# Eleven adaLN weight slabs move from the two mixer stages into the dense gate-up stage

## What is computed

```
mod = silu(c) @ w_ada[l] + b_ada[l]           # 1024 -> 6144, per sequence (1 prompt, 8 samples)
sh1, sc1, gt1, sh2, sc2, gt2 = split(mod, 6)
h = rmsnorm(x, g_mix) * (1 + sc1) + sh1
y = token_mixers(h)                            # SSD | forgetting attention | gated DeltaNet | MoBA
x = x + gt1 * (y @ w_out)
h = rmsnorm(x, g_ffn) * (1 + sc2) + sh2
x = x + gt2 * ffn(h)                           # layer 0: dense SwiGLU, layer 1: top 2 of 8 experts
```

## Time and profile before

| | us |
|---|---|
| median of 3 runs | 1411.33 |
| lowest and highest | 1409.72, 1417.41 |
| span of the profiled execution | 1419.1 |
| TensorE busy in it | 1301.8 |
| VectorE busy | 941.5 |
| ScalarE busy | 707.7 |
| time of layer 0's attention loop to the last product with the cache | about 205 to 280 |
| dense layer (gate-up, then down) | about 345 to 542 |
| layer 1's attention loop | about 713 to 780 |

### The profile page before, as it was taken

How to read it: one execution, slowest core, us unless ns; L and a number is a source line. 1 busy time by engine, 2 the same in 40 slices (tenths; PEclk the granted TensorE clock), 3 DMA queues, 4 the chain that set the end, 5 groups by cost and what they waited for, 6 DMA issues and landing times.

```text
span 1419.1 us, 25438 instructions
## 1 busy us (share of the span) xinstructions
PE 1301.8 (92%) x10487; PEld 1126.2 (79%) x10487; DVE 941.5 (66%) x1612; ACT 707.7 (50%) x1188; POOL 10.1 (1%) x22
## 2 busy tenths in 40 slices
PE   4999898987999998998888878999999999999994
PEld 3899756766999997998666657888887979797984
DVE  1675635624555545676358247898899899989986
ACT  2566222214444444563132125776677677767772
POOL 0000000000000000000000000000000000000000
PEclk9999877588999999999776888999999999999997
DMA  9545358553444443456265523898889889979991
GB/s 388 213 154 207 121 183 318 180 215 149 178 179 141 164 186 130 175 202 202 62 226 163 188 110 125 324 358 304 320 336 347 301 324 351 335 281 343 349 339 39
DMA packets 30332, 326.76 MB, mean 230 GB/s; under 512 B 6018, under 2 KB 6530, under 8 KB 8066
## 3 DMA queue, kind: packets, MB, share of 16 engines
q1 hardware_dynamic: 28738, 319.17, 61.3%
q0 software_dynamic: 1472, 5.89, 1.1%
HBM read 319.15 MB, written 5.89 MB: 229 GB/s over the span
## 4 chain that ended last, share of the span: by engine, by line
PE 81%; DVE 9%; DMA 4%; ACT 3%; issue 3%; SPq 0%; DVEq 0%; POOL 0%; ACTq 0%; POOLq 0%
PE bank L747 19%; PE bank L748 18%; PE bank L749 18%; PE bank L1132 4%; DMA ring<-in_w_ada 4%; PE bank L667 3%; PE bank L803 2%; PE bank L1226 2%; PE bank L644 1%; PE bank L699 1%; DVE w_low L2400 1%; DVE win_low L1877 1%; PE bank L1254 1%; PE bank L1005 1%; PE bank L770 1%
## 5 line engine op out<-in xcount | busy, mean ns | idle before, releaser
L2400 DVE TENSOR_TENSOR w_low<-ring,w_high 128x1024 fp32r<-128x1024 f32 x352 | 399.6, 1172 | 46.0 <-ACT w_high L1756 44.5
L1756 ACT ACTIVATE w_high<-ring 128x1024 fp32r<-128x1024 f32 x352 | 342.2, 1016 | 15.1 <-PE bank L749 13.9
L747 PE MATMUL bank<-w_high,hcH 128*128 128x512 f32 x448 | 184.9, 413 | 2.3 <-DVE w_low L2400 1.9
L749 PE MATMUL bank<-w_low,hcH 128*128 128x512 f32 x448 | 176.2, 393 | 0.0
L748 PE MATMUL bank<-w_high,hcL 128*128 128x512 f32 x448 | 176.0, 393 | 0.0
L747 PE MATMUL bank<-w_high,hidH 128*128 128x256 f32 x448 | 128.5, 287 | 3.0 <-DVE w_low L2400 3.0
L749 PE MATMUL bank<-w_low,hidH 128*128 128x256 f32 x448 | 126.7, 283 | 0.0
L748 PE MATMUL bank<-w_high,hidL 128*128 128x256 f32 x448 | 126.7, 283 | 0.0
L747 PE MATMUL bank<-pH,win_high 128*128 128x264 f32 x416 | 119.9, 288 | 2.5 <-issue 2.0
L1388 ACT ACTIVATE arena<-bank 128x264 f32<-128x264 f32 (+8 forms) x128 | 51.7, 407 | 137.7 <-PE bank L644 51.9
L748 PE MATMUL bank<-pH,win_low 128*128 128x264 f32 x416 | 117.9, 283 | 0.0
(11 more groups left out here) (393 smaller groups left out, 2548.5 us busy)
## 6 DMA issues: line engine op xcount, KB each, us to landing
ring<-in_moe_gu SPq DMA_DIRECT2D x56, 2048.0 KB, 8.6
ring<-in_moe_down SPq DMA_DIRECT2D x32, 1792.0 KB, 7.6
ring<-in_w_ada SPq DMA_DIRECT2D x24, 2048.0 KB, 8.9
ring<-in_w_in SPq DMA_DIRECT2D x16, 1536.0 KB, 6.5
ring<-in_ffn_gu SPq DMA_DIRECT2D x11, 2048.0 KB, 7.6
ring<-in_ffn_down SPq DMA_DIRECT2D x8, 1408.0 KB, 5.8
ring<-in_w_out SPq DMA_DIRECT2D x4, 2048.0 KB, 7.7
ring<-in_cache_fox_k SPq DMA_DIRECT2D x32, 128.0 KB, 3.0
```

What stands on the lines that cost most here:

```text
L747: mm(out, wh, xh, start=start, stop=False)
L749: return mm(out, wh, xl, start=False, stop=stop)
L1756: A_(split(w_high), src, ACT.Copy).then_inc(sem("w_high_ready"), 1)
L2400: TT(split(w_low), src, split(w_high), ALU.subtract).then_inc(sem("w_low_ready"), 1)
```

## The change

It takes layer 0's chunk 11 and layer 1's chunks 0 to 9 into `DENSE_ADA`: one adaLN slab behind each of the 11 gate-up slabs, in the plan and in TensorE's order. Layer 0's mixer keeps 6 slabs (gdn, chain, two at ssd, att0, att1), layer 1's keeps one (gdn). The two slabs at fixed points stay two, with other chunks. The moved slabs use PSUM banks 6 and 7, which are free in the gate-up stage. Their rows are copied by ScalarE two gate-up slabs later (`ada_copied`), turned by TensorE behind the next slab (`ada_turned`), and taken one slab after that (`ada_taken`). VectorE's `add_bias` for layer 1's first columns moves from the norm of layer 1 into the down stage. Counts of finished tiles that assumed gate-up slabs only now go through `dense_done`.

```diff
-NORM_ADA = {("ffn", 0): (1, MIX_CHUNKS - 1), ("mix", 1): (1, MIX_CHUNKS)}
-MIXER_ADA = [[(0, c) for c in range(MIX_CHUNKS, ADA_CHUNKS)] + [(1, c) for c in range(MIX_CHUNKS - 1)],
-             [(1, c) for c in range(MIX_CHUNKS + 1, ADA_CHUNKS)]]
+NORM_ADA = {("ffn", 0): (0, ADA_CHUNKS - 2), ("mix", 1): (1, ADA_CHUNKS - 2)}
+MIXER_ADA = [[(0, c) for c in range(MIX_CHUNKS, ADA_CHUNKS - 2)], [(1, ADA_CHUNKS - 1)]]
 ADA_UNITS = [
-    {"gdn": 2, "chain": 2, "ssd": 4, **{f"att{n}": 2 for n in range(7)}, "att7": 0},
-    {"gdn": 2, "chain": 2, "ssd": 2, **{f"att{n}": 2 for n in range(4)}, **{f"att{n}": 0 for n in range(4, 8)}}]
+    {"gdn": 2, "chain": 2, "ssd": 4, "att0": 2, "att1": 2, **{f"att{n}": 0 for n in range(2, 8)}},
+    {"gdn": 2, "chain": 0, "ssd": 0, **{f"att{n}": 0 for n in range(8)}}]
+DENSE_ADA = [(0, ADA_CHUNKS - 1)] + [(1, c) for c in range(ADA_CHUNKS - 2)]
...
-            out += [("gu", l, (c,), 4) for c in range(FF // 256)]
+            for c in range(FF // 256):
+                out += [("gu", l, (c,), 4), ("ada", DENSE_ADA[c][0], (DENSE_ADA[c][1],), 1)]
...
+        ada_copied = {4 * c + 8: c for c in range(FF // 256)}
+        ada_turned = {4 * c + 7: c for c in range(FF // 256)}
+        ada_taken = {4 * c + 12: c for c in range(FF // 256)}
...
                     tick(ins)
+                    if kind == "gu" and t % 4 == 3:
+                        for half in range(2):
+                            ada_unit(*DENSE_ADA[c], half, rows_in=6)
+                    if t in ada_turned:
+                        ada_turn(*DENSE_ADA[ada_turned[t]], turned_in=7)
...
                         copy(split(w_high), src, "split_high")
+                        if t in ada_copied:
+                            mod_rows(*DENSE_ADA[ada_copied[t]], rows_in=6)
+                        if t in ada_taken:
+                            mod_columns(*DENSE_ADA[ada_taken[t]], turned_in=7)
...
-                add_bias(l, 0, 4 * MIX_CHUNKS)
                 if l == 0:
+                    add_bias(l, 0, 4 * MIX_CHUNKS)
...
-                add_bias(l, 4 * MIX_CHUNKS, 48)
+                add_bias(l, *((40, 48) if l else (16, 40)))
...
+                        if t == N_GU:
+                            add_bias(0, 40, 48)
+                        if t == N_GU + 12:
+                            add_bias(1, 0, 40)
```

More of the change, by code:

```diff
@@ L123 @@
 ADA_CHUNKS = 6 * D // 512
-NORM_ADA = {("ffn", 0): (1, MIX_CHUNKS - 1), ("mix", 1): (1, MIX_CHUNKS)}
-MIXER_ADA = [[(0, c) for c in range(MIX_CHUNKS, ADA_CHUNKS)] + [(1, c) for c in range(MIX_CHUNKS - 1)],
-             [(1, c) for c in range(MIX_CHUNKS + 1, ADA_CHUNKS)]]
+NORM_ADA = {("ffn", 0): (0, ADA_CHUNKS - 2), ("mix", 1): (1, ADA_CHUNKS - 2)}
+MIXER_ADA = [[(0, c) for c in range(MIX_CHUNKS, ADA_CHUNKS - 2)], [(1, ADA_CHUNKS - 1)]]
 ADA_UNITS = [
-    {"gdn": 2, "chain": 2, "ssd": 4, **{f"att{n}": 2 for n in range(7)}, "att7": 0},
-    {"gdn": 2, "chain": 2, "ssd": 2, **{f"att{n}": 2 for n in range(4)}, **{f"att{n}": 0 for n in range(4, 8)}}]
+    {"gdn": 2, "chain": 2, "ssd": 4, "att0": 2, "att1": 2, **{f"att{n}": 0 for n in range(2, 8)}},
+    {"gdn": 2, "chain": 0, "ssd": 0, **{f"att{n}": 0 for n in range(8)}}]
+DENSE_ADA = [(0, ADA_CHUNKS - 1)] + [(1, c) for c in range(ADA_CHUNKS - 2)]
+assert len(DENSE_ADA) == FF // 256
 for _l in range(DEPTH):
@@ L456, in build, with dense_done @@
         d_out = [N_GU + 8 * (m // 2) + 6 + 2 * (m % 2) for m in range(KD)]
+        ada_copied = {4 * c + 8: c for c in range(FF // 256)}
+        ada_turned = {4 * c + 7: c for c in range(FF // 256)}
+        ada_taken = {4 * c + 12: c for c in range(FF // 256)}
+        def dense_done(t):
+            kind, a, col, z, k0, nk = D_PIECES[t]
+            return ticks_before(index[(kind, 0) + a]) + t % 4 + 1
         def dense_view(t):
@@ L585, in _ @@
             for l in range(DEPTH):
-                lo = index[("ada", l, MIX_CHUNKS)] if l else index[("in", l) + IN_SLABS[0]]
-                n_l = (index[("ada", 1, MIX_CHUNKS)] if l == 0 else n_pre) - lo
+                lo = index[("ada",) + NORM_ADA["mix", 1]] if l else index[("in", l) + IN_SLABS[0]]
+                n_l = (index[("ada",) + NORM_ADA["mix", 1]] if l == 0 else n_pre) - lo
                 for i in range(lo, lo + n_l):
@@ L657, in use, with ada_unit @@
                 return ring[slot_of[i]]
-            def ada_unit(l, c, half):
+            def ada_unit(l, c, half, rows_in=0):
                 w = ring[slot_of[index[("ada", l, c)]]][:, :].rearrange("p (k n) -> p k n", k=KD)
@@ L663, in ada_unit @@
                     use(index[("ada", l, c)])
-                b = fill(0, "mod_rows") if half == 0 else bank[0]
+                b = fill(rows_in, "mod_rows") if half == 0 else bank[rows_in]
                 for k in range(4 * half, 4 * half + 4):
@@ L670, in ada_unit, with ada_turn @@
                     tick(ins)
-            def ada_turn(l, c):
+            def ada_turn(l, c, turned_in=1):
                 o.need("mod_rows")
-                b = fill(1, "mod_ready")
+                b = fill(turned_in, "mod_ready")
                 pe.transpose(b[:, 0:P], mrow[:, :], C("ident")).then_inc(sem("mod_turned"), 1)
@@ L1397, in rms, with mod_rows, mod_columns @@
                 return A_(dst, dst, ACT.Exp, scale=-0.5)
-            def mod_rows(l, c):
+            def mod_rows(l, c, rows_in=0):
                 i = index[("ada", l, c)]
                 act_e.wait_ge(tile_done, ticks_before(i) + 1)
-                copy(mrow[:, :], bank[0][:, 0:P], "mod_rows")
-            def mod_columns(l, c):
+                copy(mrow[:, :], bank[rows_in][:, 0:P], "mod_rows")
+            def mod_columns(l, c, turned_in=1):
                 o.need("mod_turned")
-                copy(modT[:, 4 * c:4 * c + 4, :], bank[1][:, 0:P].rearrange("p (m j) -> p m j", m=4)[:, :, 0:9], "mod_ready")
+                copy(modT[:, 4 * c:4 * c + 4, :], bank[turned_in][:, 0:P].rearrange("p (m j) -> p m j", m=4)[:, :, 0:9], "mod_ready")
             def ada_drain(l, place):
@@ L1677, in _ @@
                     mod_columns(*NORM_ADA["ffn", l])
-                    t0 = ticks_before(index[("gu", 0, 0)])
                     act_e.wait_ge(sem("ffn_phase"), 1)
@@ L1687, in _ @@
                         if t >= SPLITS:
-                            act_e.wait_ge(tile_done, t0 + t + 1 - SPLITS)
+                            act_e.wait_ge(tile_done, dense_done(t - SPLITS))
                         src, split = dense_view(t)
                         copy(split(w_high), src, "split_high")
+                        if t in ada_copied:
+                            mod_rows(*DENSE_ADA[ada_copied[t]], rows_in=6)
+                        if t in ada_taken:
+                            mod_columns(*DENSE_ADA[ada_taken[t]], turned_in=7)
                         if t in f_made:
                             f = f_made[t]
-                            act_e.wait_ge(tile_done, t0 + 2 * f + 1)
+                            act_e.wait_ge(tile_done, dense_done(2 * f))
                             if f >= 2:
@@ L2277, in _ @@
                         v(TT(split(w_low), src, split(w_high), ALU.subtract), "split_low")
+                        if t == N_GU:
+                            add_bias(0, 40, 48)
+                        if t == N_GU + 12:
+                            add_bias(1, 0, 40)
                         if t in f_made:
                             f = f_made[t]
-                            ve.wait_ge(tile_done, t0 + 2 * f + 2)
+                            ve.wait_ge(tile_done, dense_done(2 * f + 1))
                             o.need("sg_ready")
@@ L2291, in _ @@
                             m = d_out.index(t - SPLITS + 1)
-                            ve.wait_ge(tile_done, t0 + d_out[m])
+                            ve.wait_ge(tile_done, dense_done(d_out[m] - 1))
                             add_x(bank[4 + m % 4], m, 40, "acc_ready", "x_whole")
```

3 lines of the change are left out of this document (removed).

## The result

The changed kernel takes 1425.36 us (median; 1419.71 to 1429.61), the kernel before beside it 1417.16 (1409.48 to 1423.17): ratio 1.0059, 95% interval 1.0041 to 1.0076, so **8.4 us slower** (5.8 to 10.8). The forecast was 10.4 us slower; its 1421.7 us for the whole was counted from 1411.33, the median of the first three of the twenty executions of the kernel before. In two later comparisons the ratios were 1.0043 (1.0013 to 1.0074) and 1.0058 (1.0029 to 1.0087).

What follows compares the result with a forecast made beforehand. TensorE's order was taken to bound the kernel, saturated in gate-up, mixed with load waits in attention. +24.1 - 8.0 - 0 - 5 - 0.5 - 0.2 = +10.4 us on 1411.33 gave 1421.7 us, range 1407 to 1429.

Steps and rivals of the forecast that it cites:

- Gate-up, +24.1: Gate-up stage: 11 moved slabs with their transposes add 2.19 us each on saturated TensorE, 24.1 us, bounds 21.2 to 26.8.
- The queue of loads at nothing: Gate-up's load ring: slabs issued later still land before TensorE needs them, so new waits cost nothing.
- cover of 2.2: Gate-up: margin of 2.2 us between copied rows at T + 11.5 and TensorE's need at T + 13.7.
- Rival 3: Gate-up: two weight slabs in the ring instead of four starve TensorE, +20 to +27 more, about 1445 us; chance 0.13.
- att5 and att6, -8.0: Layer 0's attention, last L2142 to L2193: without its two slabs the stretch is 8.0 us shorter.
- att2 to att4, 0: Layer 0's attention before L2142: removing three slabs gains 0 us as remaining work runs at the lower clock; bounds 0, 9.1.
- The wait for the shares of head 1: Layer 0's attention: TensorE waits some 2.3 us behind its own end of the scores for VectorE's shares.
- Rival 1: Freed attention loops of both layers run at the upper clock: -2.6 us in all, 1409 us; chance 0.22.
- Layer 1's attention, -5: Layer 1's att0 to att3: giving up the slabs gains 5 us, between 0 and 12.5.
- Its chain and ssd, -0.5: Layer 1 in front of the SSD: removing two slabs gains 0.5 us, between -1 and 2.2.
- The bias addition, -0.2: Norm of layer 1: the bias addition leaves it, taking 0.2 us off the chain.

Runs made afterwards that it cites:

- where five were moved: Changed kernel with only layer 0's five slabs moved into gate-up, layer 1's six left in its mixer: 1420.41 us, ratio 1.0034 to the kernel before.
- where six were: Changed kernel with only layer 1's six slabs moved into gate-up, layer 0's five left in its mixer: 1424.00 us, ratio 1.0066 to the kernel before.
- the run at an eighth: Changed kernel, each of gate-up's eleven adaLN slabs multiplied with its last k block only, loads kept: 1411.03 us, ratio 0.9982 to the kernel before.
- three blocks that load nothing: Changed kernel plus 64 matmul records on resident tokens in each of layer 0's att2 to att4: 1426.69, 1427.43 and 1423.61 us.
- blocks that load nothing: Changed kernel plus 64 matmul records on resident tokens at each of the eleven old mixer places: 1432.48 us, ratio 1.0096.
- the kernel before with eighths: Kernel before, the same eleven mixer slabs multiplied with their last k block only, loads kept: 1412.28 us, ratio 0.9978.

## Why the prediction was right, step by step

**Gate-up, +24.1: right.** 154.12 - 130.08 = 24.04, with 2.25 us a slab where five were moved and 2.18 where six were. TensorE is never idle there before an adaLN matmul, and the run at an eighth shows that its time is the price.

**The queue of loads at nothing: right.** Gate-up slabs landed 7.2, 8.6 and 10.3 us after their issue (least, median, most), against 7.3, 7.6 and 9.8; the longest is 0.5 over the bound that the prediction took, within its cover of 2.2. Rival 3 is out.

**att5 and att6, -8.0: right in mechanism, 1 us too much on the mean.** Without slabs the stretch is 20.1 us every time. With them it was 28.0 in the execution that I read, and 25.2 in another in which part of it had the upper level (0.63 instead of 0.55). I had taken the length of one execution for a constant.

**att2 to att4, 0: right.** This was the step on which the sign hung. The chain of before had 9.08 and 9.89 us of waits for loads there, and taking all three slabs out gave 0.2 us on the mean, uncertain by 1 us or more. The wait for the shares of head 1, some 2.3 us in the prediction, was 2.04 in the first trace of the changed kernel (the row at 223.67 above), and the work behind it went at the lower level. The clock is 0.57 to 0.63 without the slabs and was 0.74 to 0.80 with them. That the missing matmuls bring about the lower level is shown from the other side: three blocks that load nothing bring it to 0.83 and 0.79, and the stretch to 30.5 to 32.4 us. By the rule of the Trainium skill that the prediction set against this (TensorE: Matmul & The Clock Gate, "Why this matters for your kernels"), a loop rid of its load waits should have held the full clock; the changed kernel's rows disagree (27.32 of 28.28 us busy at 0.53), and those with blocks come nearer to it without reaching it (29.69 of 30.52 us busy at 0.83).

**Rival 1** named this same chance, the upper clock in the freed loop. It fell because the clock did not come; where blocks brought it, the stretch gained 2 to 4 us and not the 6 to 8 of the rival, since the blocks themselves take their time.

**Layer 1's attention, -5: right**, -5.6 on the mean of five against three. **Its chain and ssd, -0.5: not seen**, +0.4, less than the executions of one kernel differ there (31.8 to 34.3). **The bias addition, -0.2: not seen**; from the first down matmul to layer 1's first projection the changed kernel took 82.4 us, the kernel before 81.6, and the run with an eighth, which has the same instructions as the changed kernel there, 81.5.

**What the sum lacked.** Behind L2193 layer 0 is 3.1 us shorter without slabs, though none stood there: from 259 to 277 us the clock is at 0.79 in the changed kernel, and was 0.50 from 270 to 291 before. The window of the kernel before, and that of the changed one:

```profile
269.70:290.85 21.15, 15.51 (x68) 10.66 (x68) 15.18 (x26) 7.22 (x20) 0.00 (x0) 0.50 0.80 286
```
```profile
258.97:276.54 17.57, 11.30 (x67) 7.96 (x67) 15.08 (x26) 7.16 (x20) 0.00 (x0) 0.79 0.50 196
```

The same 67 or 68 matmuls take TensorE 15.5 us in the one and 11.3 in the other. I had ended the reading at L2193. The longer stretch goes with the matmuls of att5's and att6's slabs, not with their loads: with whole slabs there it was 21.2 us, with blocks that load nothing 20.9, and 17.6 to 19.9 in all traces without these matmuls, 17.6 among them for the kernel before with eighths, in which the loads stay. Why the clock is lower behind these matmuls no run here shows. Layer 1's 1.9 us may be of the kind, or chance, since one of three executions with slabs also had 17.6. Against that, w_out of layer 0 took 32.3 us instead of 30.6 in four executions of five. With these the table's rows come to +7.9. Outside the table, the traces have 0.7 us less from L1107 to w_out in either layer and, behind gate-up, the 0.7 more that is named above: +7.2, beside the measured 8.4. That sum and measurement lie so near is partly luck, as each of the mixer rows is uncertain by 1 us or more. The forecast of 10.4 had the same luck: it put the gain of att5 and att6 1 us and that of layer 1's chain 0.9 us too high, and left out a net gain of 3.7 us in the rows behind L2193.

## What to carry to other kernels

Before you take a wait off the chain, ask what clock the work behind it will get: a wait that vanishes at the upper level can come back as slower work at the lower one, and in a saturated stage what you took out is paid in full. Look for gaps in which the engine in question is idle with a known length, fill those, and move the hand-over to where the helper engine waits too. Read a stage with clock changes from several traces: one pair of traces gave -14 us for layer 0 here, where the mean of several gave -9.

## What the runs showed of the hardware

Adding matmuls can shorten a stretch: 192 further records in layer 0's attention loop stood in a stretch of 30.5 us that took 35.5 without them, in one pair of traces; over all traces it was 30.5 to 32.4 us with them and 32.3 to 35.5 without, and the whole kernel gained nothing on the median. The 64 records of one slab took 1.9 us at the upper level and 3.6 at the lower. And the time of one and the same program, the kernel before, goes with the mean clock that it was granted: over 106 executions 1406 us at 0.939 and 1428 us at 0.911, a spread of 1.6%, more than twice the effect of this change.
